# A two-layer decoder trunk on one core: the first stage's modulated product through one PSUM bank, two scale rows loaded ahead of the V weights, and small operations with one SBUF tensor each

## What is computed

```
mod = (silu(c) @ w_ada[l] + b_ada[l])
sh1, sc1, g1, sh2, sc2, g2 = split(mod, 6)
h = rms_norm(x, norm1_g[l]) * (1.0 + sc1) + sh1
proj = h @ w_in[l]
cb, cc, cu, q, k, v, gr = split(proj, ...)
```

## Time and profile before

| what | value |
|---|---|
| median of 3 runs | 1201.65 us |
| the profiled execution | 1203.0 us |
| its span, first to last instruction | 1201.1 us |
| PE busy | 1157.7 us, 96% of the span |
| DVE, ACT, POOL busy | 696.4, 439.7, 278.2 us |
| mean granted clock of TensorE | 0.984 of full speed |
| moved by DMA | 161.75 MB |

### The profile page before, as it was taken

How to read it: one execution, slowest core, us unless ns; L and a number is a source line. 1 busy time by engine, 2 the same in 40 slices (tenths; PEclk the granted TensorE clock), 3 DMA queues, 4 the chain that set the end, 5 groups by cost and what they waited for, 6 DMA issues and landing times.

```text
span 1201.1 us, 17245 instructions
## 1 busy us (share of the span) xinstructions
PE 1157.7 (96%) x5690; PEld 976.6 (81%) x5690; DVE 696.4 (58%) x869; ACT 439.7 (37%) x620; POOL 278.2 (23%) x193
## 2 busy tenths in 40 slices
PE   2899999999999999999999999999999999999996
PEld 1687788899888888888897888889988888888886
DVE  7799887758443434543368897766754222333333
ACT  5445444335432123432143544524543212343220
POOL 4469120132210001221113940104221000122110
PEclk7899999999999999999999999999999999999998
DMA  9655334334443353333234433333353322223212
GB/s 354 263 189 181 139 126 136 109 107 154 157 152 128 108 189 123 125 137 105 88 141 166 152 140 139 138 108 124 119 192 109 105 95 97 93 100 101 92 35 72
DMA packets 46910, 161.75 MB, mean 135 GB/s; under 512 B 5520, under 2 KB 7696, under 8 KB 46736
## 3 DMA queue, kind: packets, MB, share of 16 engines
q1 hardware_dynamic: 46864, 161.13, 38.7%
HBM read 159.01 MB, written 2.10 MB: 134 GB/s over the span
## 4 chain that ended last, share of the span: by engine, by line
PE 80%; DVE 9%; issue 6%; POOL 2%; ACT 1%; DMA 1%; SPq 0%; DVEq 0%; ACTq 0%; POOLq 0%
PE ps L306 25%; PE ps L307 25%; PE ps L308 25%; DVE ada_raw L779 3%; DVE w_lo L768 2%; PE ps L481 1%; POOL buf_a L1201 1%; DMA fin_g<-final_g 1%; PE ps L466 1%; POOL buf_b L1202 1%; DVE h_lo L971 1%; PE ps L346 0%; DVE arena L948 0%; PE ps L347 0%; PE ps L348 0%
## 5 line engine op out<-in xcount | busy, mean ns | idle before, releaser
L768 DVE TENSOR_TENSOR w_lo<-w_raw,w_hi 128x1024 fp32r<-128x1024 f32 x193 | 259.2, 1345 | 299.9 <-ACT w_hi L567 297.8
L306 PE MATMUL ps<-h_hi,w_hi 128*128 128x512 f32 (+1 forms) x960 | 363.9, 379 | 3.4 <-issue 1.8
L308 PE MATMUL ps<-h_hi,w_lo 128*128 128x512 f32 (+1 forms) x960 | 360.9, 376 | 0.0
L307 PE MATMUL ps<-h_lo,w_hi 128*128 128x512 f32 (+1 forms) x960 | 360.5, 376 | 0.0
L567 ACT CAST w_hi<-w_raw 128x1024 fp32r<-128x1024 f32 x196 | 204.6, 1046 | 244.1 <-PE ps L308 230.7
L306 PEld LDWEIGHTS ps<-h_hi,w_hi 128*128 128x128 f32 x960 | 181.1, 189 | 37.2 <-issue 2.0
L306 PE MATMUL ps<-u_hi,w_hi 128*128 128x512 f32 (+1 forms) x576 | 211.0, 366 | 0.0
L307 PE MATMUL ps<-u_lo,w_hi 128*128 128x512 f32 (+1 forms) x576 | 210.5, 365 | 0.0
L308 PE MATMUL ps<-u_hi,w_lo 128*128 128x512 f32 (+1 forms) x576 | 210.5, 365 | 0.0
L308 PEld LDWEIGHTS ps<-h_hi,w_lo 128*128 128x128 f32 x960 | 181.0, 189 | 33.0
L307 PEld LDWEIGHTS ps<-h_lo,w_hi 128*128 128x128 f32 x960 | 181.2, 189 | 32.2
(11 more groups left out here) (122 smaller groups left out, 1058.5 us busy)
## 6 DMA issues: line engine op xcount, KB each, us to landing
w_raw<-weights SPq DMA_DIRECT2D x200, 512.0 KB, 3.3
ada_raw<-ada SPq DMA_DIRECT2D x80, 512.0 KB, 4.5
arena<-ada SPq DMA_DIRECT2D x16, 512.0 KB, 14.0
x<-xT SPq DMA_DIRECT2D x2, 1024.0 KB, 6.9
outT<-x SPq DMA_DIRECT2D x8, 256.0 KB, 2.3
tab<-tables SPq DMA_DIRECT2D x1, 1024.0 KB, 16.5
tab<-tables SPq DMA_DIRECT2D x1, 512.0 KB, 15.0
ident<-identity SPq DMA_DIRECT2D x1, 64.0 KB, 2.2
```

What stands on the lines that cost most here:

```text
L306: nc.tensor.matmul(out, wh, hi, start=first, stop=False, skip_group_check=True)
L307: nc.tensor.matmul(out, wh, lo, start=False, stop=False, skip_group_check=True)
L308: return nc.tensor.matmul(out, wl, hi, start=False, stop=last, skip_group_check=True)
L768: nc.vector.tensor_tensor(w_lo[:, j, :], w_raw[:, j, :], w_hi[:, j, :].bitcast(F32), ALU.subtract).then_inc(w_lo_done, 1)
```

## The change

It touches the first stage alone.

1. **Product buffer.** The modulated product of every tile goes to one PSUM bank (`xr`, bank 4) and no longer to four SBUF buffers. `first_product(k)` therefore waits for `first_low(k - 1)`.
2. **Order of the loads.** `par` and `bia` and the first two scale rows come ahead of the V weights; `fin_g` stays behind them. The scale rows then run two ahead of the shift rows.
3. **Small operations.** The gain becomes a tensor_scalar with two per-partition scalars. The identity times `rstd` becomes four tensor_scalars of 128x128 (`first_norm`), where it was one tensor_tensor of 128x512 with two broadcast inputs.
4. **Order of work.** DVE makes `first_scale(0)` first, then `sc_bias`, `first_norm`, `first_scale(1)`, both gains, and splits V weights 0 and 3 last. ACT makes both copies of `c_act` behind the eight squares, and takes the root behind the first cast, where it was behind the second.

```
-            for j in range(SLOTS):
-                sp.dma_start(w_raw[:, j, :], weights[j, :, :]).then_inc(w_in[j], 16)
             sp.dma_start(par[:], params).then_inc(par_in, 16)
             sp.dma_start(bia[:], bias).then_inc(par_in, 16)
+            for k in range(SCALES_FIRST):
+                load_scale(k)
+            for j in range(SLOTS):
+                sp.dma_start(w_raw[:, j, :], weights[j, :, :]).then_inc(w_in[j], 16)
             sp.dma_start(fin_g[:], final_g).then_inc(par_in, 16)
...
-            first_split(1)
             norm_root(0, 1, TOKEN_TILES)
-            first_split(2)
-            first_split(3)
+            for j in (1, 2, 3):
+                first_split(j)
...
-                nc.vector.scalar_tensor_tensor(out=gm[:, 0, k:k + 1], in0=sc_sum[:, k:k + 1], scalar=sc_bias[:, k:k + 1],
-                                               in1=par[:, C_G1 + k:C_G1 + k + 1], op0=ALU.add, op1=ALU.mult
-                                               ).then_inc(gm_ready, 1)
+                nc.vector.tensor_scalar(gm[:, 0, k:k + 1], sc_sum[:, k:k + 1], sc_bias[:, k:k + 1],
+                                        par[:, C_G1 + k:C_G1 + k + 1], ALU.add, ALU.mult).then_inc(gm_ready, 1)
...
-                if k >= 4:
-                    dve.wait_ge(xs_lo, 2 * k - 6)
+                else:
+                    dve.wait_ge(xs_lo, 2 * k)
                 dve.wait_ge(gm_ready, k + 1)
-                nc.vector.scalar_tensor_tensor(out=ring[k % 4], in0=x[:, k, :], scalar=gm[:, 0, k:k + 1],
+                nc.vector.scalar_tensor_tensor(out=xr, in0=x[:, k, :], scalar=gm[:, 0, k:k + 1],
                                                in1=rinv, op0=ALU.mult, op1=ALU.mult).then_inc(xr_ready, 1)
...
-                nc.vector.scalar_tensor_tensor(out=h_lo[:, k, :], in0=ring[k % 4], scalar=mod[:, 2 * k:2 * k + 1],
+                nc.vector.scalar_tensor_tensor(out=h_lo[:, k, :], in0=xr, scalar=mod[:, 2 * k:2 * k + 1],
...
+            def first_norm():
+                dve.wait_ge(norm_std, 1)
+                nc.vector.reciprocal(rstd[:], std[:]).then_inc(norm_r, 1)
+                dve.wait_ge(norm_r, 1)
+                for t in range(TOKEN_TILES):
+                    mm = nc.vector.tensor_scalar(ssum[:, t * P:(t + 1) * P], ident[:], rstd[:, t:t + 1], None, ALU.mult)
+                mm.then_inc(norm_r, 1)
+
+            dve.wait_ge(c_ready, 2)
+            first_scale(0)
+            dve.wait_ge(par_in, 48)
+            nc.vector.tensor_scalar(sc_bias[:], bia[:, 1:2 * KT:2], 1.0, None, ALU.add).then_inc(sc_summed, 1)
+            first_norm()
+            first_scale(1)
+            first_gain(0)
+            first_gain(1)
             first_split(0)
-            norm_scale(0, 1, TOKEN_TILES)
-            first_scale(0)
-            first_gain(0)
             first_split(3)
-            first_scale(1)
-            first_gain(1)
```

More of the change, by code:

```diff
@@ L47 @@
 HALF_TILES = 16
+SCALES_FIRST = 2
 U_V, U_QK, U_HEAD, U_OUT = 0, 4, 12, 28
@@ L169, in trunk @@
         squared = [ps[:, i, :] for i in range(4)]
+        xr = ps[:, STAT, :]
         c_in, par_in, rope_in, decay_in = sem("c_in"), sem("par_in"), sem("rope_in"), sem("decay_in")
@@ L247, in _, with load_scale @@
                              ).then_inc(x_in[i], 16)
+            def load_scale(k):
+                sp.dma_start(arena[:, 2 * k + 1, :], ada[2 * k + 1, :, :]).then_inc(sc_in[k], 16)
+            sp.dma_start(par[:], params).then_inc(par_in, 16)
+            sp.dma_start(bia[:], bias).then_inc(par_in, 16)
+            for k in range(SCALES_FIRST):
+                load_scale(k)
             for j in range(SLOTS):
                 sp.dma_start(w_raw[:, j, :], weights[j, :, :]).then_inc(w_in[j], 16)
-            sp.dma_start(par[:], params).then_inc(par_in, 16)
-            sp.dma_start(bia[:], bias).then_inc(par_in, 16)
             sp.dma_start(fin_g[:], final_g).then_inc(par_in, 16)
-            for i in range(KT):
-                sp.dma_start(arena[:, 2 * i, :], ada[2 * i, :, :]).then_inc(sh_in[i], 16)
-                sp.dma_start(arena[:, 2 * i + 1, :], ada[2 * i + 1, :, :]).then_inc(sc_in[i], 16)
+            for k in range(KT):
+                sp.dma_start(arena[:, 2 * k, :], ada[2 * k, :, :]).then_inc(sh_in[k], 16)
+                if k + SCALES_FIRST < KT:
+                    load_scale(k + SCALES_FIRST)
             sp.wait_ge(w_lo_done, 2 * SLOTS)
@@ L630, in _ @@
                 nc.scalar.activation(squared[m % 4] if m else ssum[:], x[:, m, :], ACT.Square).then_inc(x_squared, 1)
[L631 to L634, removed]
+            for i in range(2):
+                act.wait_ge(c_ps, i + 1)
+                nc.scalar.copy(c_act[:, HALVES_D[i]], ps[:, 6 + i, :]).then_inc(c_ready, 1)
             def first_split(j):
@@ L652, in first_high @@
                 act.wait_ge(sh_ready, k + 1)
-                nc.scalar.activation(h_hi[:, k, :], ring[k % 4], ACT.Identity, bias=mod[:, 2 * k:2 * k + 1]
+                nc.scalar.activation(h_hi[:, k, :], xr, ACT.Identity, bias=mod[:, 2 * k:2 * k + 1]
                                      ).then_inc(xs_hi, 2)
             first_split(0)
-            first_split(1)
             norm_root(0, 1, TOKEN_TILES)
-            first_split(2)
-            first_split(3)
+            for j in (1, 2, 3):
+                first_split(j)
             act.wait_ge(par_in, 48)
@@ L940, in _ @@
                                         ).then_inc(x_added, 1)
-            dve.wait_ge(par_in, 48)
-            nc.vector.tensor_scalar(sc_bias[:], bia[:, 1:2 * KT:2], 1.0, None, ALU.add).then_inc(sc_summed, 1)
-            dve.wait_ge(c_ready, 2)
             def first_scale(k):
```

## The result

The changed kernel took 1203.66 us (median of 14 runs, 1202.15 to 1204.12); the kernel before, beside it, 1200.98 us (1199.91 to 1201.97). The ratio is 1.002, with a 95% interval of 1.0013 to 1.0026: 1.6 to 3.1 us slower. The forecast was 1203.15 us, 1.5 us more than before.

A forecast was written before the change was run, and what follows sets the result against it. PE, busy 96% of the span, bounds the kernel; only its wait in the first stage can give. V's start +6.2 and course -4.7 make +1.5 us on 1201.65, so 1203.15 us, range 1195.6 to 1206.3.

The forecast's parts named there:

- The lock: First stage: DVE operations between SBUF tensors stand still until POOL's operation ends; h_lo took 2.90 us against 0.74.
- Part 1, the product in PSUM: V projection: h_lo no longer held, 2.85 us a tile, V's course 23.9 us instead of 28.6, a gain of 4.7.
- Part 2, when POOL begins: Load order: fin_g lands at 18.7 us, POOL's first split begins at 17.35, sc_bias is held to 19.7.
- the first hold: DVE's sc_bias, waiting for fin_g until 18.7 us, then held by POOL's first split to 19.7.
- Part 3, the norm in four: DVE's norm: POOL wins each turn, so the four tensor_scalars run from about 19.9 to about 29.4 us.
- the two reasons given for it: Why POOL wins the norm's turns: the tensor_scalars have a per-partition scalar to read first, and start after POOL.
- Rival A: Norm in four: DVE keeps the port through all four; V ends at 56.0, 1196.4 us; chance 0.18 in full.
- What is left to the first matmul: Gains, splits, product 0 and h_lo 0 after the norm: PE begins V at 38.9 us, where it was 32.67.
- Rival B: DVE's gains are held by POOL too; V ends at 65.5, 4.2 us later than before, 1205.9 us; chance 0.13.
- Rival C: h_lo is held all the same, costing under 1 us, 1204.1 us; chance 0.07 together with others.
- The sum: End of V at 62.8 against 61.27 us, 1.5 later (start +6.2, course -4.7); median 1203.15 us.
- the chances: Whole kernel: faster by over 0.2% 0.27, slower 0.27, within 0.2% 0.46; the forecast itself 0.50.

The follow-up runs named there:

- four alone: The kernel before with only the norm in four tensor_scalars of 128x128; loads, order, gains and product buffers as before: 1204.12 us, ratio 1.0026.
- norm in one: The changed kernel with the norm as one tensor_tensor of 128x512 again: 1197.25 us, ratio 0.997.
- fin_g first: The changed kernel with the load of fin_g moved directly behind par and bia, ahead of the scale rows: 1194.77 us, ratio 0.9947.
- PSUM alone: The kernel before with only the product in the PSUM bank; loads, order, norm and gains as before: 1197.43 us, ratio 0.9976.
- PSUM and gain: The kernel before with the product in the PSUM bank and the gain as tensor_scalar: 1194.74 us, ratio 0.9949.
- four tensor_tensors: The changed kernel with the four norm operations as tensor_tensors of 128x128, rstd broadcast: 1203.81 us, ratio 1.0023.
- norm from PSUM: The changed kernel with the identity copied to PSUM by ACT and read there by the four tensor_scalars: 1196.53 us, ratio 0.9962.
- loads in front: The kernel before with product in PSUM, gain as tensor_scalar, and par, bia, fin_g loaded ahead of the V weights: 1192.66 us, ratio 0.9931.

## Why the prediction came out right, step by step

- **The lock.** Right. `sc_bias`, the norm, the splits and the h_lo on SBUF buffers, where they started while POOL worked, ended at POOL's end plus their own time: `sc_bias` at 19.66, with 19.7 forecast. Two small operations between SBUF tensors were not held: the gain as a tensor_scalar (one element, 0.27) and the reciprocal (four elements, 0.18).
- **Part 1, the product in PSUM.** The mechanism is right: h_lo takes 0.74, a tile 2.89 (2.85 forecast). **What it was said to be worth is wrong.** "This part gives 4.7 us" books the whole shortening of V's course to the product buffer. With the four alone, and no product in PSUM, the course is 24.15 us, 4.4 shorter than before: the late begin of V shortens it. In the kernel before, where V begins early, the buffer alone shortens the course by 2.2 us, and the freed gains are needed as well for 24 us. That it moved the end of V by 4.4 us there, near the forecast 4.7, is luck, since half of it came from V's begin. All parts but the norm in four together bring 3.6 us with the norm in one operation (ratio 0.997), and nothing that can be told from zero with the norm in four.
- **Part 2, when POOL begins.** Right. fin_g lands at 18.47 (18.7), POOL's first split starts at 17.29 (17.35). The condition named there ("fin_g landing before 17 us ... would take the first hold away") was tried, and it is worth 8.9 us between the medians (1203.66 and 1194.77), from a load of 4 KB.
- **Part 3, the norm in four.** The size is right: 19.78 to 28.92, where 19.9 to about 29.4 was forecast. **Of the two reasons given for it, one was not needed.** Four operations without a scalar lose their turns just as well. The other, that POOL starts ahead, holds in every one of these turns. Where DVE was slightly ahead instead, the rows still divide as the prediction read them, splits winning and h_lo losing. Rival A fell: in the three kernels whose four operations stood beside POOL (9.14, 9.06 and 9.36 us), none of them kept the port for a second one.
- **What is left to the first matmul.** 38.42 for 38.9; the chain was a few tenths shorter all along.
- **Rival B**, held gains, fell: two gains take 0.45 us beside POOL's product. The Trainium skill, in "Advanced Engine Details and Errata", Mode Summary, leaves a single element out of the two-port forms; the trace agrees, with 0.27 us for each gain, while 8 elements at `sc_bias` were held.
- **Rival C** fell: no h_lo beside POOL takes over 0.75.
- **The sum.** +1.5 was forecast and 1.6 to 3.1 measured, so the forecast lies just under the interval, and the ratio of 1.002 lies on the line that the chances drew between "within 0.2%" and "slower". That the time itself is only 0.5 off is in part luck: the base was the median 1201.65, and the kernel before took 1200.98 this time. The undersized term is V's course. It was taken as 23.9 from a stretch with one slow begin of 8 matmuls, and it is 24.34 in the mean of nine executions. With it, V ends at 38.4 + 24.3 = 62.7, 1.6 behind 61.1. The forecast end, 62.8, is as near as that because its begin was 0.5 too late and its course 0.4 too short.

About a microsecond is left. Over the ten executions of changed kernels, the measured difference of time is above the difference of V's end by this much:

| kernel | end of V less 61.1 | time, by the ratio | the rest |
|---|---|---|---|
| after, its two profiles | +1.0, +2.3 | +2.4, +3.4 | 1.4, 1.1 |
| norm in one | -5.1 | -3.6 | 1.5 |
| fin_g first | -7.0 | -6.4 | 0.6 |
| PSUM alone | -4.4 | -2.9 | 1.5 |
| four alone | +1.9 | +3.1 | 1.2 |
| PSUM and gain | -7.5 | -6.1 | 1.4 |
| four tensor_tensors | +2.0 | +2.8 | 0.8 |
| norm from PSUM | -4.7 | -4.6 | 0.1 |
| loads in front | -9.7 | -8.3 | 1.4 |

The rest is 0.1 to 1.5 us, 1.1 in the mean, for edits that made the kernel faster as for those that made it slower. It thus belongs to no part of the change. The runs show where most of it comes from: the two profiled executions of before, from which 61.1 is taken, took longer than is usual for their kernel: 1203.0 and 1201.3 us, 2.0 and 0.5 above the medians 1200.98 and 1200.77. The first took longer than any of the timed runs of that kernel (1202.64 at most). The ten profiled executions of changed kernels lie 0.95 below to 0.88 above their medians, 0.1 below in the mean. Take their mean excess of 1.3 us from the comparison, and the rest is near zero in the mean (an estimate). Whether a usual execution of before saves it in V or behind V is not shown.

Behind V there is one place that differs from profile to profile. In layer 2, near 640 us, PE waits for about 2 us in every profile of before and after, and in some its clock then falls for a while. After's first profile reads 0.79 from 640 to 644 us and 0.78 from 644 to 648, its second 1.00 in both. The kernel before, too, has a profile with the dip and one without. In the profiles in which the clock holds, PE's longest wait for q_lo behind it is 1.1 us (after) and 1.3 us (before), in those with the dip 0.2 us or none, so the dip costs little in the end. From the first product behind V to the end the profiles take 1137.6 and 1138.9 us with before, and 1137.5 to 1138.6 with all others, after among them. That shows no difference between the kernels behind V.

## What to carry to other kernels

While GpSimd works through large SBUF operations, cutting a VectorE operation between SBUF tensors into four made four waits of about 2.3 us out of one here. Put such operations ahead of GpSimd's first one, or move one operand into PSUM; don't cut one up beside it. A small load on which all of them wait (4 KB here, behind six others of 512 KB) decides on which side of GpSimd's start they fall. And before a gain is booked to an edit, look at whether the delay beside it brings the same gain: a late begin of V made its course as short as the freed h_lo did.

## What the runs showed that had not been expected

- The same four operations took 0.87 us ahead of POOL, 1.12 beside it with an operand in PSUM, and 9.14 beside it with both in SBUF.
- With POOL 0.04 to 0.12 us ahead, it won every turn against the four, with a per-partition scalar or without one. With DVE 0.01 to 0.03 ahead, the splits won all nine turns and h_lo none of six.
- The norm in four, alone, took as long as the whole change: V's course fell from 28.6 to 24.15 us without any of the other parts.
- How long PE stays at the pace of the lower clock after its wait differs from one execution to the next: 7 to 14 matmuls, 1.5 to 2.9 us in all. Two profiles of one kernel therefore differ by up to 1.4 us at the end of V, about as much as the whole effect in question.
